# First adaLN modulation by blocks of 256 features on TensorE, first two in-projection tiles k-tile by k-tile, rotary sines moved into layer 0

## Chip, cores and metric

The kernel runs on one core of a Trainium2 chip. The metric is the device time of one execution, in microseconds (us). Before the change it is 2322.17 us, the median of three runs (2317.86 to 2325.34).

## What is computed

A decoder trunk of two layers over x (1024 tokens of 1024 features, f32). Cut to what the change touches, the reference is:

```
c_act = silu(c)                                    # 1024 values
for l in range(2):
    mod = c_act @ ada_w[l] + ada_b[l]              # 6 x 1024 values
    sh1, sc1, g1, sh2, sc2, g2 = split(mod, 6)
    h = rmsnorm(x, norm1_g[l]) * (1.0 + sc1) + sh1
    proj = h @ w_in[l]                             # in-projection, 20 tiles of 128 columns
    ...                                            # SSD, latent attention (rotary keys), window attention
    x = x + g1 * (y @ w_out[l])
    ...                                            # gated channel mixer
cos, sin = cos/sin(positions * inv_freq)           # for the rotary key and queries
```

Before the first in-projection tile can run, the kernel needs: x transposed, the inverse root mean square of each token, sh1 and sc1 of layer 0 (two column blocks of `ada_w[0]`, 8 MB), and the first tiles of `w_in`.

## The kernel before

The program is one block with five queues (SP issues the DMAs, TensorE, VectorE, ScalarE, GpSimd), each a hand-written order with semaphore waits. `first` fills the queues up to the first in-projection tile, `trunk_layer` follows once per layer; there is no barrier between them.

Every large matmul takes its operands as two fp32r parts, high and low (`wHi`, `wLo`, `hHi`, `hLo`), and makes three products (high by high, high by low, low by high). ScalarE writes the high part of a weight tile and GpSimd the low part (`split_ahead` for tiles 0 and 1, `split_pre` for the others). Tokens are the moving columns: two halves of 512.

`first` before the change:

- SP loads c, the rotary constants, eight x tiles (L539), then sixteen tiles of `ada_w[0]` (L536, 128 rows of 4 KB each: eight of sc1, then eight of sh1), then `w_in` tile 1. At its end it waits for the sines and stores cos and sin (L546).
- GpSimd fills constants, issues the loads of the positions, the parameters and `w_in` tile 0, and makes the low parts of tiles 0 and 1.
- TensorE transposes x (L595), the parameters (L434 to L439), takes four of the sixteen `ada_w` tiles as weights against one column of c_act (L603), and spreads the inverse norms into `bank[2]` (`spread_rms`, L480).
- ScalarE evacuates the x transposes (L623), squares x for the norms (L636), and makes the sines (L638, L644).
- VectorE works out the rotary angles (L662 to L673), multiplies and adds the other twelve `ada_w` tiles (L687, L690), folds them (L695, L696), and makes `mod` and `scl` (L680, L681, L703).

`trunk_layer` of layer 0 then makes h for the first 512 tokens, k-tile by k-tile: VectorE `nt = xT * scl * spread` (L2204, the spread read from PSUM), ScalarE `hHi` (L1807), VectorE `hLo` (L2213); then the same for the other 512 tokens. TensorE (L1184) runs in-projection tiles 0 and 1 on the first half, then on the second; tile 2 and the others follow by `dense_step` (L1124), over all 1024 tokens. Tile m uses `bank[m % 2]`, and TensorE waits on `pair_free0`/`pair_free1` until it is evacuated. For tiles 0 to 3 ScalarE alone evacuates. For tiles 4 to 11 ScalarE writes the convolution's base (L1874) and VectorE adds three taps from the bank (L2331), and only then the bank is free: so tile 6 waits for the taps of tile 4.

VectorE's own order in layer 0 after `hLo`: `early_products(0)` (the third modulation vector, eight tiles, L2265 and L2268), `step_sum`, `step_sizes` (which waits for a logarithm of ScalarE), `mod_fold(0)`, `early_products(1)`, `mod_fold(1)`, and then the taps of tile 4.

Of the kernel before, what the change touches and what calls it, by code (L numbers as in the profile page):

```python
# [129 lines left out]
ADA_BY_PE = (3, 7, 11, 15)  # L130
ADA_BY_DVE = (0, 1, 2, 4, 5, 6, 8, 9, 10, 12, 13, 14)
X_ACT = 8
# [46 lines left out]
def pv_end(u):  # L179
# [16 lines left out]
    "ada_prod": 14, "dve_step": 75, "n1_sq": 16, "n1_acc": 14, "n1_sum": 2, "n1_rstd": 4, "n1_spread": 2, "n1_scaled":  # L196
    24, "n1_hi": 24, "n1_lo": 24, "n2_sq": 16, "n2_acc": 14, "n2_sum": 2, "n2_rstd": 4, "n2_spread": 2, "n2_scaled": 16,
# [19 lines left out]
    "x_transposed": ("up_silu", NB), "x_copied_act": ("up_mul", X_ACT), "x_copied_dve": ("g_sums", NB - X_ACT),  # L217
    "c_transposed": ("dn_c", 1), "c_act": ("dn_copied", 1), "angle": ("dn_u", 1), "rope_sin": ("dn_pre", 2),
    "ada_done": ("dn_used", 14), "ada_sum": ("us_c", 6), "cs_stored": ("cum_loaded", 128)}
FIRST_ON.update({f"mod_loaded{i}": (name, 16) for i, name in enumerate(  # L220
    "dc_loaded0 dc_loaded1 dc_loaded2 g_stored0 g_stored1 g_stored2 x_back x_saved tail_loaded0 tail_loaded1 "
    "sd_row_stored sd_spread uproj_loaded cum_stored dt_stored dt_loaded".split())})
FIRST = {"dve_step": 16, "params_transposed": 1, "params_copied": 4, "mod_first": 2, "next_loaded1": 16, "next_hi": 2, "next_lo": 2, "next_swap": 2,
# [7 lines left out]
def build(nc, x, c, positions, ada_w, ada_b, norm1_g, norm2_g, w_in, ssd_conv_w, ssd_conv_b,  # L231
# [169 lines left out]
    def fview(t):  # L401
        return t.bitcast(F32)
# [87 lines left out]
    xin = [place(f"xin{i}", [P, D], F32, E[i]) for i in range(NB)]  # L490
    crow = place("crow", [8, P], F32, E[8])
    posi = place("posi", [P, T], I32, E[10])
    adaw = [place(f"adaw{i}", [P, D], F32, at["h"] + 4 * K * i) for i in range(2 * KT)]
    adas = [place(f"adas{g}", [P, D], F32, E[12 + g]) for g in range(2)]
    foldP = place("foldFirst", [P, 2, 32], F32, E[15])
# [27 lines left out]

    def first(block):

        def first_sums(a):

            return bank[3][:, 16:16 + 3 * KT] if a else bank[0][:, 0:3 * KT]

        @block.sync  # L530
        def _(sp):
            sp.dma_start(crow[:], c.rearrange("b (k p) -> (b k) p", p=P)).then_inc(s["small_loaded"], 16)
            sp.dma_start(ropec[:], rope_consts).then_inc(s["small_loaded"], 16)
            def load_adaw(i):
                g, k = 1 - i // KT, i % KT
                sp.dma_start(adaw[i][:], ada_w[0, k * P:(k + 1) * P, g * D:(g + 1) * D]).then_inc(s[f"mod_loaded{i}"], 16)  # L536
# [3 lines left out]
            for i in range(2 * KT):  # L540
                load_adaw(i)
# [2295 lines left out]
```

## Time and profile before

| | |
|---|---|
| Median of three runs | 2322.17 us |
| Span of the profiled execution | 2319.9 us |
| TensorE matmul busy | 2259.9 us (97%) |
| VectorE, ScalarE, GpSimd busy | 1633.3, 1102.8, 1021.4 us |
| First in-projection matmul | 47.85 us |
| Tile 2 begins | 72.40 us |

Times in the rows are microseconds from the start of the span. PE is TensorE's matmuls, PEld its weight loads, DVE VectorE, ACT ScalarE, POOL GpSimd, SPq the queue of SyncE. A row of a timeline gives start, duration, engine, line, operation and the tiles written and read; merged rows end with their count. The duration of an instruction that was held back while it ran includes that time. PEclk is the granted TensorE clock as a share of full speed (1.00 is 2.4 GHz, 0.50 is 1.2 GHz).

### The profile page before, as it was taken

The page shows a single profiled execution, that of the slowest core. Times are in us where ns is not written, and L with a number is a line of the kernel's source. Part 1 is how long each engine was busy: PE and PEld are TensorE (multiplying, and loading weights), DVE is VectorE, ACT ScalarE, POOL GpSimd, SP SyncE. Part 2 cuts the span into 40 slices and gives each one's busy share as a digit, 9 for nine tenths or more (in the row PEclk, how much of TensorE's full clock was granted, in tenths as well). Part 3 has the DMA queues.
Part 4 walks back from the last instruction along what each step waited for, and adds up shares of the span by engine and source line. Part 5 has one row for each costly group of instructions (what it writes and reads, how often), then busy time and mean ns, then how long its engine had stood idle before and what let it go on. Part 6 is the DMA issues. An engine that isn't in the chain of part 4 may idle for free.

```text
span 2319.9 us, 31032 instructions
## 1 busy us (share of the span) xinstructions
PE 2259.9 (97%) x11401; PEld 1853.4 (80%) x11401; DVE 1633.3 (70%) x2098; ACT 1102.8 (48%) x1817; POOL 1021.4 (44%) x660
## 2 busy tenths in 40 slices
PE   7999999999999999999999999999999999999998
PEld 6888867887788888888878787778878888888887
DVE  7985468449867666778888744772796767667886
ACT  5355557434444444444543464772454444444455
POOL 3222368445887777300012224053389777760000
PEclk7999999999999999999999999999999999999999
DMA  9742243242333333487466131114323333347763
GB/s 329 283 129 70 63 118 119 110 136 64 103 120 97 116 98 107 161 279 256 146 219 242 54 87 55 37 38 164 119 63 106 114 91 114 91 136 259 256 207 114
DMA packets 271301, 317.13 MB, mean 137 GB/s; under 512 B 33613, under 2 KB 188032, under 8 KB 270383
## 3 DMA queue, kind: packets, MB, share of 16 engines
q1 hardware_dynamic: 269359, 312.11, 41.7%
q10 hardware_dynamic: 1072, 2.23, 0.5%
q8 instruction: 91, 1.49, 0.3%
q0 software_dynamic: 720, 0.81, 0.1%
q14 instruction: 59, 0.48, 0.1%
HBM read 248.37 MB, written 62.54 MB: 134 GB/s over the span
## 4 chain that ended last, share of the span: by engine, by line
PE 84%; DVE 7%; issue 3%; ACT 2%; DMA 1%; SPq 1%; POOL 1%; DVEq 0%; ACTq 0%; POOLq 0%
PE bank L1561 31%; PE bank L1124 19%; PE bank L1576 17%; PE bank L1184 6%; PE bank L1343 1%; PE bank L1424 1%; DVE hLo L2227 1%; PE bank L1452 1%; ACT swaProb L1948 1%; SPq L536 1%; DVE xT L2221 1%; DMA adaw<-in_ada_w_dram 1%; PE bank L1274 1%; DVE xT L2562 1%; DVE tLo L2631 1%
## 5 line engine op out<-in xcount | busy, mean ns | idle before, releaser
L1044 POOL TENSOR_TENSOR wLo<-raw,wHi 128x1024 fp32r<-128x1024 f32 x66 | 161.2, 2443 | 408.6 <-ACT wHi L1046 408.6
L1754 POOL TENSOR_TENSOR prodLo<-comb,prodHi 128x512 fp32r<-128x512 f32 x160 | 233.9, 1468 | 122.4 <-ACT prodHi L1086 122.4
L1561 PE MATMUL bank<-tHi,prodHi 128*128 128x512 f32 x640 | 250.5, 391 | 4.8 <-DVE tLo L2631 4.1
L1561 PE MATMUL bank<-tLo,prodHi 128*128 128x512 f32 x640 | 250.0, 391 | 0.0
L1561 PE MATMUL bank<-tHi,prodLo 128*128 128x512 f32 x640 | 249.8, 390 | 0.0
L1576 PE MATMUL bank<-gateHi,downHi 128*128 128x512 f32 x616 | 240.6, 391 | 0.0
L1576 PE MATMUL bank<-gateHi,downLo 128*128 128x512 f32 x616 | 240.0, 390 | 0.0
L1576 PE MATMUL bank<-gateLo,downHi 128*128 128x512 f32 x616 | 239.9, 390 | 0.0
L1086 ACT ACTIVATE prodHi<-comb 128x512 fp32r<-128x512 f32 x160 | 100.5, 632 | 248.9 <-PE bank L1561 231.2
L2576 DVE SCALAR_TENSOR_TENSOR ub<-bank,ffp,ub 128x1023 f32<-128x1023 f32 x88 | 112.8, 1282 | 141.8 <-ACT ub L2034 140.2
L1561 PE MATMUL bank<-hHi,prodHi 128*128 128x512 f32 x480 | 187.3, 390 | 6.3 <-POOL prodLo L1754 3.7
L1561 PE MATMUL bank<-hHi,prodLo 128*128 128x512 f32 x480 | 187.0, 390 | 0.0
L1561 PE MATMUL bank<-hLo,prodHi 128*128 128x512 f32 x480 | 187.0, 390 | 0.0
L1124 PE MATMUL bank<-hHi,wHi 128*128 128x512 f32 x576 | 184.9, 402 | 0.0
L1124 PE MATMUL bank<-hLo,wHi 128*128 128x512 f32 x576 | 178.3, 391 | 0.0
L1124 PE MATMUL bank<-hHi,wLo 128*128 128x512 f32 x576 | 177.5, 390 | 0.0
L1046 ACT ACTIVATE wHi<-raw 128x1024 fp32r<-128x1024 f32 x66 | 69.6, 1057 | 219.9 <-PE bank L1124 144.9
L1754 POOL TENSOR_TENSOR prodLo<-raw,prodHi 128x512 fp32r<-128x512 f32 x120 | 164.7, 1398 | 0.0
L1561 PEld LDWEIGHTS bank<-tHi,prodHi 128*128 128x128 f32 x640 | 120.5, 188 | 31.5 <-DVE tLo L2631 5.0
L1561 PEld LDWEIGHTS bank<-tHi,prodLo 128*128 128x128 f32 x640 | 120.6, 188 | 25.2
L1561 PEld LDWEIGHTS bank<-tLo,prodHi 128*128 128x128 f32 x640 | 120.6, 188 | 24.7
L1576 PEld LDWEIGHTS bank<-gateHi,downHi 128*128 128x128 f32 x616 | 115.7, 188 | 24.7 <-issue 0.8
(424 smaller groups left out, 5434.9 us busy)
## 6 DMA issues: line engine op xcount, KB each, us to landing
raw<-in_ffn_w_up_dram SPq DMA_DIRECT2D x88, 512.0 KB, 4.7
gateRaw<-gateOut SPq DMA_DIRECT2D x154, 256.0 KB, 4.2
adaE<-in_ada_w_dram SPq DMA_DIRECT2D x64, 512.0 KB, 6.6
gateOut<-gateSums SPq DMA_DIRECT2D x22, 1024.0 KB, 5.5
raw<-in_w_in_dram SPq DMA_DIRECT2D x34, 512.0 KB, 4.1
downRaw<-in_ffn_w_down_dram SPq DMA_DIRECT2D x66, 256.0 KB, 3.6
raw<-in_w_out_dram SPq DMA_DIRECT2D x28, 512.0 KB, 3.8
downCols<-in_ffn_w_down_dram SPq DMA_DIRECT2D x24, 512.0 KB, 3.7
```

The costliest lines, as they stand in the source:

```text
L536: sp.dma_start(adaw[i][:], ada_w[0, k * P:(k + 1) * P, g * D:(g + 1) * D]).then_inc(s[f"mod_loaded{i}"], 16)
L1044: eng.tensor_tensor(lo[:], raw[slot][:], fview(hi[:]), ALU.subtract).then_inc(s["split_lo"], 1)
L1046: eng.activation((early_hi if n in (N_OUT0, N_PRE + 2) else third_hi if n == 2 else wHi[slot])[:], raw[slot][:], ACT.Copy).then_inc(s["spl ...
L1086: act.activation(sHiW[idx][:], product_source(js, idx), ACT.Copy).then_inc(s["us_hi"], 1)
L1124: last = mm(half(pair, hf), w(k), r(k)[:, HALF * hf:HALF * (hf + 1)], start=first and q == 0, stop=last_k and q == 2)
L1184: last = mm(o, w[n % 2][:, k * P:(k + 1) * P], r(k)[:, cols], start=first and q == 0, stop=last_k and q == 2)
L1274: last = mm(o, xd[:, h, :], Mt[g][:, q, :], start=True, stop=True)
L1343: last = mm(half(to, hf), wuq[:, k, t, :], cq[:, k, HALF * hf:HALF * (hf + 1)], start=k == 0, stop=k == 1)
L1561: last = mm(o, w[idx][:, c0], moving(idx, kp, hi), start=kp == 0 and q_ == 0, stop=kp == 3 and q_ == 2)
L1576: last = mm(down_bank(p, m), w[ring(n)][:, m * P:(m + 1) * P], g[ring(n)][:], start=i == 0 and q == 0, stop=i == NK - 1 and q == 2)
L1754: pool.tensor_tensor(sLoW[idx][:], product_source(js, idx), fview(sHiW[idx][:]), ALU.subtract).then_inc(s["us_lo"], 1)
L2576: dve.scalar_tensor_tensor(out=y[:, d:T], in0=bank[2 * q + b][:, 0:T - d], scalar=ffp[:, col:col + 1], in1=y[:, d:T], op0=ALU.mult, op1=AL ...
```

## The change

- **Loads.** The sc1 and sh1 parts of `ada_w[0]` come as eight transfers of 1 MB (all 1024 rows, 256 features, 1 KB pieces), sc1 block 0, sh1 block 0, then `w_in` tile 1, then blocks 1 to 3. The positions are loaded after `w_in` tile 0.
- **Modulation.** TensorE multiplies c_act, broadcast to 32 columns, by each block (`mod_products`: 16 plain f32 matmuls of 256 columns for a pair of blocks, each written to one of four groups of 32 partitions). ScalarE copies the sums out (`mod_rows`), TensorE transposes them (`mod_columns`), and VectorE reduces and adds the bias for two k-tiles of `mod` and `scl`. This goes four times; the first is in `first`, the other three stand inside the first two in-projection tiles.
- **h.** `xhat = x * spread` is made once for all 1024 tokens: k-tiles 0 to 3 by VectorE from PSUM, 4 to 7 by GpSimd from a copy in `nt[2]`. Then ScalarE makes `hHi` from it with scale and bias, and VectorE `nt = xhat * scl` and `hLo`.
- **Tiles 0 and 1** run over k-tiles, both tiles and both halves at each k, with the products of the next block after tile 0 of k = 0, 2, 3 and its transposes after tile 1.
- **Evacuation of the x transposes** goes from ScalarE to VectorE.
- **Sines.** The angles are worked out by VectorE after the last `hLo`, ahead of `early_products(0)`; the sines by ScalarE before its tile 2; the store of cos and sin stands before SP's `w_in` tile 5. `w_in` tiles 2 and 3 are issued before the wait for the modulation.

```diff
+    def mod_products(pe, b):
+        for n, g in enumerate(MOD_ORDER):
+            pe.wait_ge(s[f"mod_loaded{2 * b + n}"], 16)
+            if b:
+                pe.wait_ge(s["mod_row"], 2 * b)
+            for k in range(KT):
+                j = k % 4
+                last = pe.matmul(bank[3][32 * j:32 * j + 32, 256 * g:256 * g + 256], cact[:, k:k + 1].to_broadcast([P, 32]), adaw[g][b][:, k, :],
+                                 start=k < 4, stop=k >= 4)
+            last.then_inc(s["mod_made"], 1)
...
         @block.gpsimd
-            for n in range(AHEAD):
-                split_ahead(pool, n)
+            pool.dma_start(posi[64:128, :], positions.to_broadcast([64, T])).then_inc(s["pos_loaded"], 16)
+            split_ahead(pool, 0)
+            pool.wait_ge(s["spread_copied"], 1)
+            for k in range(X_BY_DVE, KT):
+                if k == X_BY_DVE + 1:
+                    split_ahead(pool, 1)
+                pool.tensor_tensor(xhat[k][:], xT[:, k, :], nt[2][:], ALU.mult).then_inc(s["xhat_pool"], 1)
...
         @block.scalar
+            act.wait_ge(s["n1_spread"], 1)
+            act.wait_ge(s["xhat_dve"], 2)
+            act.activation(nt[2][:], bank[2][:], ACT.Copy).then_inc(s["spread_copied"], 1)
             split_ahead(act, 0)
+            for b in range(MOD_BLOCKS):
+                mod_rows(b)
+                if b == 0:
+                    split_ahead(act, 1)
+                act.wait_ge(s["mod_first"], b + 1)
+                for k in range(2 * b, 2 * b + 2):
+                    act.wait_ge(s["xhat_dve" if k < X_BY_DVE else "xhat_pool"], k + 1 if k < X_BY_DVE else k + 1 - X_BY_DVE)
+                    act.activation(hHi[:, k, :], xhat[k][:], ACT.Identity, bias=mod[:, k:k + 1], scale=scl[:, 0, k:k + 1]).then_inc(s["n1_hi"], 1)
...
         @block.vector
+            for b in range(MOD_BLOCKS):
+                dve.wait_ge(s["mod_turned"], b + 1)
+                link(dve.tensor_reduce(both, bank[3][:, HALF:T].rearrange("p (g i j r) -> p g i j r", g=2, i=2, j=4)[:, :, :, :, 0], AX.X, ALU.add))
+                link(dve.tensor_tensor(both, both, prm[:, R_ADAB:R_ADAB + 2 * KT].rearrange("p (g k) -> p g k", g=2)[:, :, cols], ALU.add))
+                dve.scalar_tensor_tensor(out=scl[:, 0, cols], in0=mod[:, KT + 2 * b:KT + 2 * b + 2], scalar=1.0, in1=prm[:, R_N1 + 2 * b:R_N1 + 2 * b + 2],
+                                         op0=ALU.add, op1=ALU.mult).then_inc(s["mod_first"], 1)
+                for k in range(2 * b, 2 * b + 2):
+                    dve.tensor_scalar(nt[k % 2][:], xhat[k][:], scl[:, 0, k:k + 1], None, ALU.mult).then_inc(s["n1_scaled"], 1)
+                for k in range(2 * b, 2 * b + 2):
+                    dve.wait_ge(s["n1_hi"], k + 1)
+                    dve.scalar_tensor_tensor(out=hLo[:, k, :], in0=nt[k % 2][:], scalar=mod[:, k:k + 1], in1=fview(hHi[:, k, :]),
+                                             op0=ALU.add, op1=ALU.subtract).then_inc(s["n1_lo"], 1)
...
+            if not layer:
+                for k in range(KT):
+                    for t in range(2):
+                        pe.wait_ge(s["n1_lo"], nth("n1_lo", k + 1))
+                        last = dense_step(t, k, tile_of(t, wHi), tile_of(t, wLo), h_hi, h_lo, k == 0, k == KT - 1)
+                        if k in MOD_AT:
+                            (mod_columns if t else mod_products)(pe, MOD_AT.index(k) + 1)
...
-            for hf in range(1 if layer else 0, 2):
-                if layer:
-                    dve.wait_ge(s["n1_spread"], nth("n1_spread", 0))
-                norm1_apply(hf, n1_done(hf, -1), begun=not hf)
+            if layer:
+                dve.wait_ge(s["n1_spread"], nth("n1_spread", 0))
+                norm1_apply(1, n1_done(1, -1))
+            else:
+                rope_angles(dve, link)
```

## Rows read from the trace of the kernel before

**Rows 1.** The page, part 1: busy time, share of the span, instructions

```profile
PE 2259.9 (97%) x11401; PEld 1853.4 (80%) x11401; DVE 1633.3 (70%) x2098; ACT 1102.8 (48%) x1817; POOL 1021.4 (44%) x660
```

**Rows 2.** Chain of waits of the first 330 us: start, us, what

```profile
24.47 16.56 DMA adaw<-in_ada_w_dram
41.08 3.58 PE bank L603 x16
...
47.85 24.71 PE bank L1184 x96
72.56 62.56 PE bank L1124 x276
```

**Rows 3.** Stretches: length, busy of each engine, PEclk, DMA share, GB/s

```profile
24.00:26.00 2.00, 0.91 (x7) 0.71 (x9) 1.77 (x2) 2.00 (x5) 0.00 (x0) 0.72 1.02 406
...
52.00:54.00 2.00, 2.00 (x9) 1.60 (x9) 1.93 (x4) 0.86 (x2) 0.00 (x0) 0.95 1.02 395
```

**Rows 4.** DMA issues at 5.6 to 6 and 6 to 7 us: size, us to landing

```profile
xin<-in_x_dram SPq DMA_DIRECT2D x1, 512.0 KB, 12.6
...
adaw<-in_ada_w_dram SPq DMA_DIRECT2D x2, 512.0 KB, 15.3
```

**Rows 5.** Timeline of TensorE, first stage: start, us, engine, line, operation

```profile
21.29 1.06 PE L595 MATMUL bank<-ident,xin 128*128 128x128 f32 x8 [0.89 <-ACT xT L623]
...
34.32 1.97 PE L480 MATMUL bank<-ident,rst 128*128 128x128 f32 x8 [0.60 <-DVE rst L699]
```

**Rows 6.** Groups by line and shape: busy us, mean ns of one

```profile
L2460 DVE TENSOR_TENSOR swaProb<-bank,band 128x1024 f32<-128x1024 f32 x14 | 17.1, 1220 | 4.0 <-PE bank L1383 3.7
...
L687 DVE TENSOR_SCALAR adas<-adaw,cact 128x1024 f32<-128x1024 f32 x2 | 1.5, 748 | 0.0
...
L476 ACT ACTIVATE wHi<-raw 128x1024 fp32r<-128x1024 f32 x4 | 4.2, 1054 | 10.7 <-DMA raw<-in_w_in_dram 10.6
```

**Rows 7.** Timelines of VectorE and GpSimd at 69 to 79 us

```profile
68.94 0.75 DVE L2265 TENSOR_SCALAR nt<-adaE,cact 128x1024 f32<-128x1024 f32 x1
...
69.72 3.30 DVE L2268 SCALAR_TENSOR_TENSOR nt<-adaE,cact,nt 128x1024 f32<-128x1024 f32 x1
73.06 1.28 DVE L2268 SCALAR_TENSOR_TENSOR nt<-adaE,cact,nt 128x1024 f32<-128x1024 f32 x1
...
69.10 2.84 POOL L1044 TENSOR_TENSOR thirdLo<-raw,thirdHi 128x1024 fp32r<-128x1024 f32 x1 [23.12 <-DVE hLo L2213]
75.61 2.39 POOL L1044 TENSOR_TENSOR wLo<-raw,wHi 128x1024 fp32r<-128x1024 f32 x1 [3.66 <-ACT wHi L1046]
```

**Rows 8.** The same timelines at 562 to 569 us, both queues full

```profile
563.38 2.77 DVE L2569 SCALAR_TENSOR_TENSOR xT<-xT,mod 128x512 f32<-128x512 f32 x1
566.07 2.89 DVE L2562 TENSOR_TENSOR xT<-xT 128x512 f32<-128x512 f32 x1
...
562.76 8.46 POOL L1758 TENSOR_TENSOR tLo<-xT,tHi 128x1024 fp32r<-128x1024 f32 x3
```

**Rows 9.** Timeline of TensorE: plain f32 matmuls, output 128, 64, 32 wide

```profile
195.30 0.60 PE L1260 MATMUL bank<-xbc 128*128 128x128 f32 x4
...
197.95 1.09 PE L1274 MATMUL bank<-Mt,xdt 128*64 128x128 f32 x16 [0.67 <-DVE Mt L2377]
...
178.86 0.31 PE L1201 MATMUL bank<-foldMod,quadSum 128*32 128x32 f32 x8
```

**Rows 10.** Timeline of VectorE: first and last of 10 angle operations

```profile
12.59 0.69 DVE L663 CAST nt<-posi 64x1024 f32<-64x1024 int32 x1
...
22.52 0.69 DVE L673 TENSOR_SCALAR nt<-nt 64x1024 f32<-64x1024 f32 x1
```

**Rows 11.** Timeline of VectorE in layer 0, and tile 5's stretch

```profile
87.24 0.22 DVE L2244 TENSOR_SCALAR cs<-cs 64x128 f32<-64x128 f32 x1 [4.01 <-ACT cs L1902]
...
108.69 3.91 DVE L2331 SCALAR_TENSOR_TENSOR xbc<-bank,prm,xbc 128x1023 f32<-128x1023 f32 x3
...
105.04:115.92 10.88, 10.88 (x50) 9.02 (x48) 10.65 (x9) 2.16 (x2) 2.40 (x1) 1.00 0.72 255
```

## Prediction made before the change was run

> **What bounds the kernel now.** I read the page's busy shares first, then the chain of waits, then the timelines of the first 120 us. TensorE is busy for 97% of the span [rows 1], and from the first in-projection matmul on the chain stays on it: tiles 0 and 1 from 47.85 us, tile 2 from 72.40 us [rows 2] (the chain merges its first matmul, its piece begins at 72.56). So a microsecond won or lost before tile 2 is one of the whole, if nothing gives way later. Ahead of 47.85 us the chain is a DMA: the last `ada_w` tile lands at 41.08 us, and its matmuls, VectorE's fold and the first h follow [rows 2]. That is what the change attacks. The profiled span is 2319.9 us, the median of the runs 2322.17, so 2.3 us are added to a sum made on the span. About 7 us (0.3%) is what a measurement of this kernel can tell from no change.
>
> **Part 1: up to the first matmul.** The last x tile is issued at 5.4 us and lands 12.6 us later, at about 18.1 [rows 4]. Its pair is transposed in 2 x 1.06 us [rows 5], to 20.2; VectorE copies the last one out of PSUM (1.22, as for any 1024 columns read there [rows 6]), to 21.7. The parameter transposes take about 1.3 us (0.9 to 1.7 by the clock), to 23, and the eight spreads 1.0 to 2.0 [rows 5]: spread ready at 24.4 (23.6 to 25.4). The first two `ada_w` tiles land at 21.4 (6.1 + 15.3 [rows 4]) and the sixteenth at 41.08 [rows 2], that is 1.31 us for each 512 KB, so block 0 (2 MB) is there at about 25. Its products take 3.4 us at half clock (part 2), to 28.5; the clock is 0.72 at 24 to 26 us, already falling [rows 3].
>
> Meanwhile VectorE makes xhat 0 and 1 (2 x 1.25), to 26.9; ScalarE copies the spread (1.05 [rows 6]), to 28.1, and splits tile 0 (1.6 with its two small copies), to 29.7. Then come the rows (0.7) and TensorE's four transposes, to 31.9, and the reduce, to 32.1. GpSimd makes the low part of tile 0 (2.39 [rows 7]) until 32.2.
>
> **Now the new wait.** From 32.2 GpSimd has five operations in its queue: xhat 4, low part of tile 1, xhat 5, 6, 7, each two SBUF tensors of 1024 columns, so 2.39 us each [rows 7]. VectorE needs five before `hLo` 0 is done: bias add and scl (0.18 each), two `tensor_scalar` (0.78 with the gap, [rows 6]) and `hLo` (1.31 with the gap [rows 7]), all on SBUF alone. Such operations exclude each other here: a 1.28 us operation of VectorE lasted 3.30 while GpSimd's ran, and GpSimd's own, begun under a 0.75 us `tensor_scalar`, lasted 2.84 instead of 2.39 [rows 7]. With both queues full they take turns: 0.75 us operations of VectorE lasted 2.77 and 2.89, and three of GpSimd 8.46 [rows 8]. So four of GpSimd's five go between VectorE's: 32.2 + 4 x 2.39 + 2 x 0.18 + 2 x 0.78 + 1.31 = 45.0 us for the first matmul. Without turns it would be 35.6. Before it was 47.85. The gain here is 2.9 us (by the spread's bounds 1.9 to 3.7; by another phase of the turns down to -1), not 12.
>
> The Trainium skill ("SBUF — State Buffer", section "SBUF: two separate sides") says the same from the other side: one port pair of VectorE and GpSimd is an exclusive lock, held for the whole instruction, asked for by a VectorE operation with two SBUF inputs or in its 2-port mode. It speaks against this change, which puts five GpSimd operations where VectorE's chain stands. Were the two `tensor_scalar` free of it, contrary to the page, the first matmul would come at 38.7.
>
> **Part 2: tiles 0 and 1.** Before, they took 24.55 us (47.85 to 72.40), 96 matmuls with the first 4 us at half clock [rows 2, 3]. The same matmuls and the same ramp remain, now with these in the queue:
> - Three times 16 plain f32 matmuls of 256 columns with 32 output partitions. A plain f32 matmul is two instructions. With 128 output partitions, those of 128 columns come every (0.60 - 0.27) / 3 = 0.11 us; with 64, in alternate halves, 16 take 1.09, one per 0.055; with 32, in four groups, eight of 32 columns begin within 0.08 us, which is one per 0.012 [rows 9] (0.27 and 0.23 are the lengths of one). So groups run beside each other. At 256 columns one alone is 0.213. Four at once: 32 / 4 x 0.213 = 1.7 us a block. Two at once 3.4, one after another 6.8. I take 1.7, since the row with four groups is of this form; 3.4 is the upper end. Cost 3 x 1.7 = 5.1 us (up to 10.2).
> - Three times four transposes, 0.5 each: 1.5 us.
> - After the first block's transposes VectorE needs about 3.6 us (0.6, two 0.78, 1.31) before k-tile 2, and TensorE has 2.7 us of k-tile 1: 0.9 us idle. Later blocks are ahead.
>
> Sum 32.05, so tile 2 begins at 77.05, not 72.40: +4.65 us. ScalarE and GpSimd split tile 2 after `hLo` 7 (about 71), within 3.5 us: in time.
>
> The Trainium skill ("TensorE: Matmul & The Clock Gate", section "Part 3: Packing small matmuls — row/col tiling") measured 2.38 times for three column tiles, not 3. By an estimate from that page a block would be 2.1 us and tile 2 would begin 1.2 us later still.
>
> **Part 3: the sines in layer 0.** The angle operations take 10.6 us on VectorE (12.59 to 23.21 [rows 10]). They ran while the loads were awaited, but VectorE's chain after them was as long as the loads. Now they stand between `hLo` 7 and `early_products(0)`. Queued behind them: both early products, `step_sum` (for which ScalarE then waits at tile 2, about one us past its next split), the step sizes, and the taps of tile 4, for which TensorE waits at tile 6. Before, the taps ended at 112.6 and tile 6 began at 115.92 [rows 11]: 3.3 us of slack. The balance, relative to the start of tile 2: +10.6 angles; -2.7, as `hLo` 7 ends 6.1 us ahead of tile 2 and not 3.4; -2.4, as VectorE no longer idles 4.01 us for the logarithm [rows 11] but about 1.6; +4.2 for two more splits of GpSimd (tiles 4 and 5 or 6) which now meet VectorE busy with two SBUF inputs, 2.1 each (3.30 - 1.28 [rows 7]); -3.3 slack. Stall at tile 6: 6.4 us (2 without the meetings, 8.5 if the idle time stays). Once tile 6 is delayed, each later tile gives VectorE 10.88 us [rows 11] for about 9 of work, so I expect it once only. ScalarE's two sine operations and a table load (about 3.5 us) stand before its split of tile 4, where it waited for TensorE: 0 us, up to 1 if the angles come late. SP: the store of cos and sin waits for the sines and `w_in` tile 5 stands behind it, needed some 20 us later: 0. The earlier issue of tiles 2 and 3: 0, neither was waited for; it puts `ada` loads of layer 0 behind the modulation, 20 us later than before, still ahead of VectorE.
>
> **Sum.** 2319.9 - 2.85 + 7.5 + 6.4 = 2331.0 on the span; with 2.3 around it 2333 us, that is +11.
>
> **Rivals.**
> 1. *Not slower: the turns don't happen at the start and the lag is absorbed.* GpSimd's operations would have to fall between VectorE's instead of ahead of each. First matmul at 35.6, tile 2 at 67.6, no stall: -4.8 us, 2317.4. It decides from a first matmul earlier than 40.4 us with no idle at tile 6. If besides the clock stayed full (the ramp costs some 2 us), 2315. For it: [rows 3] shows the clock lost only where TensorE was sparse. Against it: [rows 7, 8].
> 2. *No turns at the start, but the lag.* 2317.4 + 6.4 = 2323.8. For it: the operations at the start have small ones among them, which may slip through.
> 3. *Turns at the start, lag absorbed.* 2322.17 + 4.65 = 2326.8. For it: 2.4 us of VectorE's slack at the logarithm and 3.3 at tile 6; it needs GpSimd's splits to miss VectorE.
> 4. *Column groups run two at a time.* Block 0 at half clock takes 6.8, the first matmul comes at 47.4, and three blocks cost 5.1 us more: 2333.2 + 7.5 = 2340.7. For it: the pair row; against it: the row with four groups [rows 9].
>
> **How the numbers follow.** Forecast 50%, own range 2329 to 2337; rival 1: 7%; rival 2: 13%; rival 3: 15%; rival 4: 13%; 2% for what I have not seen. The range of 8 in 10 leaves out most of rival 1 and the top of rival 4: 2319 to 2341. Faster by over 0.3% (below 2315.2): the best tail of rival 1 and something unseen, 6%. Slower by over 0.3% (above 2329.1): 47 of the forecast's 50, rival 4, and 2 of the others: 62%. Within: 32%.
>
> **What would show it.** Right: GpSimd's xhat operations back to back from about 32 us with VectorE's 0.18 and 0.75 us operations lasting 2.4 to 3.2 between them; first matmul at 45; tile 2 at 77; products of a block in 1.7 us; an idle of some 6 us of TensorE before tile 6, ended by VectorE's third tap of tile 4. Wrong: a first matmul before 41 (part 1), products of 3.4 us (part 2), no idle before tile 6 (part 3). A spread later than 26 us would move everything with it.

## The result, and the profile after

The changed kernel takes 2341.03 us (median of four runs, 2338.88 to 2342.15) against 2322.18 us before: a ratio of 1.0082, 95% interval 1.0068 to 1.0096, or +19 us. The prediction was 2333 (+11) with a range of 2319 to 2341, so the sign was right and the size was 8 us short. The profiled execution has a span of 2337.1 us, 17.2 more than the one before.

TensorE's busy time hardly moved. This is the page, part 1 (it answers to [rows 1]):

```profile
PE 2251.4 (96%) x11465; PEld 1839.2 (79%) x11465; DVE 1630.6 (70%) x2085; ACT 1099.1 (47%) x1811; POOL 1032.4 (44%) x664
```

So the 17 us are idle time and slow clock, and it is enough to look for TensorE's waits. The chain of waits of the changed kernel answers to [rows 2] (start, us, what):

```profile
64.64 9.59 PE bank L1138 x42
74.25 1.04 ACT misc L1917
75.31 13.79 DMA dtOut<-misc
89.11 2.48 DMA cs<-dtOut
...
106.08 11.42 DMA adaE<-in_ada_w_dram
...
136.05 9.02 PE bank L1138 x30
```

Before, one piece of TensorE ran from 72.56 us on. Now the chain leaves TensorE at 74 us and comes back at 136. Two kinds of DMA stand in it that the chain before did not have: a 32 KB store of dt that took 13.8 us, with its reload, and a late load of the fourth modulation vector. The timeline of TensorE shows the three places where it stood (first matmul of tiles 0, 3 and 6), and the first matmul of tile 2:

```profile
42.23 1.19 PE L1138 MATMUL bank<-hHi,wHi 128*128 128x512 f32 x2 [12.73 <-DVE hLo L717]
...
75.42 0.70 PE L1138 MATMUL bank<-hHi,thirdHi 128*128 128x512 f32 x2
...
94.00 1.22 PE L1138 MATMUL bank<-hHi,wHi 128*128 128x512 f32 x2 [7.41 <-POOL wLo L1058]
...
136.05 1.19 PE L1138 MATMUL bank<-hHi,wHi 128*128 128x512 f32 x2 [6.68 <-DVE xbc L2364]
```

Each stall also costs clock. By stretches (length, busy of TensorE, PEclk, DMA share, GB/s):

```profile
94.00:98.00 4.00, 4.00 (x10) 0.50 0.00 0
98.00:100.00 2.00, 2.00 (x8) 0.70 0.90 203
...
136.00:140.00 4.00, 3.95 (x9) 0.50 1.05 315
```

After these waits of 7.4 and 6.7 us, TensorE runs at half clock (1.2 GHz) for 4 to 5 us. From tile 3's first matmul (94.00) to tile 6's turn (136.05 - 6.68 = 129.37) three tiles took 35.4 us; at 10.88 each [rows 11] they need 32.6: 2.7 us for the clock. After tile 6 it is 2.1: a fixed set of products later (`foldMod`, 178.86 us before) starts 65.0 us after tile 6's first matmul, before the change 62.9.

| | before | after | difference |
|---|---|---|---|
| First in-projection matmul | 47.85 | 42.23 | -5.6 |
| Tile 2 begins | 72.40 | 75.42 | +3.0 |
| Stall at tile 3, and its clock | 0 | 7.4 + 2.7 | +10.1 |
| Stall at tile 6, and its clock | 0 | 6.7 + 2.1 | +8.8 |
| `foldMod` products begin | 178.86 | 201.05 | +22.2 |
| Layer 1, `swaV` transposes | 1436.93 | 1457.17 | +20.2 |
| Span | 2319.9 | 2337.1 | +17.2 |

The terms give 3.0 + 10.1 + 8.8 = 21.9 of the 22.2. The last two rows of the table say that 2 us come back between 201 and 1457 us and 3 after that. The 3 are the clock of these two executions: over the 63 us from the `swaV` transposes of layer 1 the granted clock was 0.92 before (1437 to 1500 us) and 1.00 after (1457 to 1520 us), which is 5 us. Where the 2 are I have not found; both are of the size by which runs differ.

### The profile page after: what moved, and what is told of

Read it like the earlier page. It is cut to its first block, busy times and chain, and to the rows that moved or that the text cites. A ratio compares the mean times of both kernels' runs of the same rounds, so it can differ in the third digit from the quotient of the medians.

```text
span 2337.1 us, 31167 instructions
## 1 busy us (share of the span) xinstructions
PE 2251.4 (96%) x11465; PEld 1839.2 (79%) x11465; DVE 1630.6 (70%) x2085; ACT 1099.1 (47%) x1811; POOL 1032.4 (44%) x664
## 4 chain that ended last, share of the span: by engine, by line
PE 81%; DVE 8%; issue 3%; ACT 3%; DMA 2%; POOL 1%; SPq 1%; DVEq 0%; ACTq 0%; POOLq 0%
PE bank L1588 30%; PE bank L1138 17%; PE bank L1603 17%; PE bank L1198 5%; PE bank L1370 1%; PE bank L1451 1%; DVE hLo L2257 1%; ACT swaProb L1979 1%; PE bank L1479 1%; DVE xT L2251 1%; DMA raw<-in_ffn_w_up_dram 1%; PE bank L1288 1%; DVE xT L2595 1%; DMA dtOut<-misc 1%; DVE tLo L2664 1%
## 5 line engine op out<-in xcount | busy, mean ns | idle before, releaser
L1058 POOL TENSOR_TENSOR wLo<-raw,wHi 128x1024 fp32r<-128x1024 f32 x66 | 161.8, 2452 | 431.4 <-ACT wHi L1060 431.4
L1138 PE MATMUL bank<-hHi,wHi 128*128 128x512 f32 x608 | 198.1, 407 | 27.4 <-DVE hLo L717 13.3
L1138 PE MATMUL bank<-hLo,wHi 128*128 128x512 f32 x608 | 190.3, 394 | 0.0
L1138 PE MATMUL bank<-hHi,wLo 128*128 128x512 f32 x608 | 189.0, 392 | 0.0
L1138 PEld LDWEIGHTS bank<-hHi,wHi 128*128 128x128 f32 x608 | 111.4, 191 | 50.4 <-issue 21.7
L1588 PEld LDWEIGHTS bank<-tLo,prodHi 128*128 128x128 f32 x640 | 120.2, 188 | 24.6
```

The costliest lines, as they stand in the source:

```text
L1058: eng.tensor_tensor(lo[:], raw[slot][:], fview(hi[:]), ALU.subtract).then_inc(s["split_lo"], 1)
L1138: last = mm(half(pair, hf), w(k), r(k)[:, HALF * hf:HALF * (hf + 1)], start=first and q == 0, stop=last_k and q == 2)
L1588: last = mm(o, w[idx][:, c0], moving(idx, kp, hi), start=kp == 0 and q_ == 0, stop=kp == 3 and q_ == 2)
```

## Where the waits come from: reading the trace

The row `[7.41 <-POOL wLo L1058]` says that GpSimd's low part of tile 3 ended the wait. GpSimd had itself waited for ScalarE's high part, and ScalarE for a DMA of its own. ScalarE's timeline after the change:

```profile
75.31 0.57 ACTq L1921 DMA_DIRECT2D dtOut<-misc  x1
...
89.11 0.53 ACTq L1924 DMA_DIRECT2D cs<-dtOut  x1
89.75 1.06 ACT L1060 ACTIVATE wHi<-raw 128x1024 fp32r<-128x1024 f32 x1 [12.79 <-DMA dtOut<-misc]
```

and before:

```profile
71.62 0.55 ACTq L1890 DMA_DIRECT2D dtOut<-misc  x1
...
73.51 0.52 ACTq L1893 DMA_DIRECT2D cs<-dtOut  x1
74.47 1.06 ACT L1046 ACTIVATE wHi<-raw 128x1024 fp32r<-128x1024 f32 x1 [0.84 <-issue]
```

The same store took 1.9 us before and 13.8 now. What had changed around it is in the timeline of SP's queue. After:

```profile
65.27 3.96 SPq L845 DMA_DIRECT2D adaE<-in_ada_w_dram  x8
69.28 0.44 SPq L888 DMA_DIRECT2D xtail<-xT  x1
...
97.30 3.90 SPq L576 DMA_DIRECT2D csOut<-cs  x8
...
101.95 4.61 SPq L845 DMA_DIRECT2D adaE<-in_ada_w_dram  x8
```

and before:

```profile
46.03 3.90 SPq L835 DMA_DIRECT2D adaE<-in_ada_w_dram  x8
...
55.86 3.28 SPq L876 DMA_DIRECT2D xtail<-xT  x1
...
78.53 3.88 SPq L835 DMA_DIRECT2D adaE<-in_ada_w_dram  x8
```

SP waits for `mod_first`, the signal that the modulation of layer 0 is made, ahead of eight loads (`adaE`, the third modulation vector, 4 MB). Before, that wait ended at 46 us; now the last block of the modulation is made at 65, so these loads and the 4 MB save of x behind them (`xtail`) start 5 to 10 us before ScalarE's 32 KB store. The second group of `adaE` loads, for the fourth vector, stands behind the store of cos and sin, that behind the sines, those on ScalarE behind the dt round trip: 101.95 us instead of 78.53.

My theory after reading this: (1) the stall at tile 3 is the dt store behind the 8 MB; (2) the stall at tile 6 is the late loads of the fourth vector. The rival for (2) was the prediction's own: VectorE's lag from the angle operations.

## The experiments

Stalls are read from TensorE's timeline or waits of each profile; "at 2322" is the ratio's excess times 2322 us. All compare with the kernel before.

| | change made to | ratio (95%) | at 2322 | tile 2 begins | stall tile 3 | stall tile 6 |
|---|---|---|---|---|---|---|
| the change | | 1.0082 (1.0068-1.0096) | +19 | 75.42 | 7.4 | 6.7 |
| e1 | change: saves early | 1.0046 (1.0032-1.0061) | +10.7 | 76.12 | 0 | 6.0 |
| e2 | change: split first | 1.0106 (1.0093-1.0119) | +24.6 | 73.90 | 0 (4.3 at tile 4) | 13.7 |
| e3 | change: no angles | 1.0096 (1.0083-1.0110) | +22.3 | 75.37 | 6.5 | 7.5 |
| e4 | change: xhat on VectorE | 1.0080 (1.0068-1.0092) | +18.6 | 66.75 | 7.9 | 11.2 |
| e5 | before: saves late | 1.0030 (1.0015-1.0046) | +7.0 | 71.69 | 0 (0.8 at tile 4) | 5.0 |
| e6 | e1, no angles | 1.0034 (1.0023-1.0045) | +7.9 | 75.12 | 0 | 3.8 |
| e7 | e6, cos/sin store last | 1.0014 (1.0004-1.0024) | +3.3 | 76.44 | 0 | 0 |
| e8 | change: all mended | 0.9993 (0.9982-1.0004) | -1.6 | 67.11 | 0 | 0.3 |
| e9 | change: dt on GpSimd | 1.0103 (1.0088-1.0118) | +23.9 | 75.03 | 0.8 (0.9 at tile 4) | 15.4 |
| e10 | change: save of x early | 1.0056 (1.0044-1.0069) | +13.0 | 74.52 | 0 | 8.6 |

**e1: SP's save and early loads ahead of its wait.**

```diff
                         load_pack(3, kind, 3)
-                        sp.wait_ge(s["mod_first"], nth("mod_first", 0))
-                    load_early(0, range(KT), 0)
+                        sp.wait_ge(s["x_copied"], NB)
+                        sp.dma_start(xtail, xT[:]).then_inc(s["tail_saved"], 16)
+                        load_early(0, (0, 1, 2, 3, 5, 6, 7), 0)
+                        sp.wait_ge(s["mod_turned"], MOD_BLOCKS)
+                        load_early(0, (4,), 0)
...
```

> The changed kernel, with SP's 4 MB save of x and its eight loads of the third modulation vector issued before its wait for the whole first modulation (some 45 us) instead of after it (65.3 to 69.7 us). Theory: TensorE's 7.4 us at tile 3 are ScalarE's wait for its own 32 KB store of dt, which took 13.8 us because 8 MB were queued ahead of it; the store should land in about 2 us, the split of tile 3 come at about 77 instead of 89.8, and the 7.4 us go. The 6.7 us at tile 6 should go too, since the early loads of the fourth vector, which they wait for, are issued some 12 us sooner (at most 1 us left by VectorE's own queue): 2341.0 - 7.4 - 6.7 = 2327, bounds 2326 to 2329. Rival A, the sum of the prediction, in which VectorE's lag behind the angle operations makes the stall at tile 6 by itself: 7.4 go, 6.4 stay, 2334. Rival B, the store of dt is slow for another reason: no change, 2341.

Measured: 1.0046. Tile 3 no longer waits; from ScalarE's, VectorE's and TensorE's timelines of e1:

```profile
76.01 0.56 ACTq L1926 DMA_DIRECT2D dtOut<-misc  x1
...
77.86 0.52 ACTq L1929 DMA_DIRECT2D cs<-dtOut  x1
78.49 1.06 ACT L1065 ACTIVATE wHi<-raw 128x1024 fp32r<-128x1024 f32 x1 [0.84 <-DMA dtOut<-misc]
...
107.44 0.75 DVE L2301 TENSOR_SCALAR nt<-adaE,cact 128x1024 f32<-128x1024 f32 x1 [1.04 <-DMA adaE<-in_ada_w_dram]
...
125.96 0.77 PE L1143 MATMUL bank<-hHi,wHi 128*128 128x512 f32 x1 [6.04 <-DVE xbc L2369]
```

The store is back at 1.9 us and the first part of the theory holds. The second does not: the loads of the fourth vector were issued 10 us sooner (91.57) and tile 6 still waited 6.0 us. Rival A, the prediction's sum, came out in size: +10.7 for +11, and 6.0 us of stall for 6.4. But the loads are not out of the way in e1. VectorE was free for the fourth vector's products at 106.4 us and waited 1.04 us more for their loads, so the loads set the 6.0, and VectorE's own lag stands just behind them, at about 5.0. That the two are so close is a coincidence. What I had missed is the difference between e1 and the change.

**e3: without nine of the angle operations** (cos and sin are not the reference's).

```diff
-        link(dve.tensor_scalar(ang[lo, :], ang[lo, :], ropec[lo, 0:1], None, ALU.mult))
-        ...
-        link(dve.tensor_scalar(ang[lo, :], ang[lo, :], ropec[lo, 2:3], None, ALU.add))
```

> The changed kernel without nine of the eleven angle operations on VectorE (the conversion and the last clamp stay; 8.3 us less work; the angles, and so cos and sin, are not the reference's). Theory: in the changed kernel VectorE waits 9.5 us for the loads of the fourth vector after this work, so taking it away moves nothing: tile 3 waits 7.4, tile 6 waits 6.7, 2341 within 1 us. Rival, the step of the prediction (VectorE's lag behind the angles makes the stall at tile 6): the stall at tile 6 goes, 2334.5.

Measured: 1.0096, no gain; 6.5 and 7.5 us of stall, as the theory said. VectorE, 9 us earlier at the products of the third vector, waited 5.95 us for those loads (to 78.8 us) and then 10.0 us for the fourth's. So neither e1, which makes the loads 10 us sooner, nor e3, which takes the angles out, changes the stall at tile 6 by as much as 1 us. Two causes side by side would do that: whichever is reduced, the other is as late.

**e6 and e7: both causes removed.** e6 is e1 with e3's edit; e7 also moves the store of cos and sin behind the fourth vector's loads:

```diff
-                if kind == "win" and m == 5 and not layer:
+                if kind == "win" and m == 6 and not layer:
                     store_rope(sp)
```

> e1_saves_early, also without nine of the eleven angle operations (so cos and sin are not the reference's). In e1 TensorE still waited 6.0 us at tile 6; VectorE began the products of the fourth vector at 107.4, 1.0 us after it was free and when its loads had landed. Theory (two causes of about the same size stand behind the wait at tile 6, VectorE's lag and the loads of the fourth vector, issued behind the store of cos and sin): with the lag gone the loads alone remain, which move up by the 3 us that the sines waited for the angles: 2 to 4 us of wait at tile 6, 2329 to 2331. Rival (the lag alone): no wait, 2327.

> e6, with SP's store of cos and sin moved behind the loads of the fourth vector. Theory of two causes: both are gone, no wait at tile 6 and none at tile 3: e1 minus 6.0, that is 2327. Rival (the tile waits for something else, for instance ScalarE or the weight loads): a wait of 2 us or more stays.

Measured: 3.8 us of stall in e6, none in e7; 1.0034 and 1.0014. VectorE's timelines show the step from one to the other: in e6 it still stood 7 us for the loads, in e7 not at all.

```profile
104.22 0.75 DVE L2292 TENSOR_SCALAR nt<-adaE,cact 128x1024 f32<-128x1024 f32 x1 [7.05 <-DMA adaE<-in_ada_w_dram]
```

```profile
98.41 0.75 DVE L2292 TENSOR_SCALAR nt<-adaE,cact 128x1024 f32<-128x1024 f32 x1
```

What remains of the change in e7, +3.3 us, is of the size of tile 2's later start (76.44 - 72.40 = 4.0). The run that has the lag alone, e1 with the store of cos and sin last and the angles kept, was not made; the 5.0 us above are read from e1's trace.

**e2: ScalarE splits tile 3 before it waits for the dt store.**

```diff
                     if m == 1:
+                        if not layer:
+                            split_pre(act, 3)
                         act.wait_ge(s["dt_stored"], nth("dt_stored", 16))
...
-                        split_pre(act, 3)
+                        if layer:
+                            split_pre(act, 3)
```

> The changed kernel, with ScalarE's split of tile 3 ahead of its wait for the store of dt in layer 0. Both theories: the 7.4 us of TensorE at tile 3 go, the store of dt still takes about 13.8 us. Theory: what follows on ScalarE (sines, store of cos and sin by SP, then the loads of the fourth vector) stays where it is in time, so tile 6 waits for what it waited for, now 7.4 us longer: a stall of 13 to 14 us at tile 6, the time within 1.5 us of 2341. Rival: the two stalls are independent, the one at tile 6 stays 6.7, 2333.6.

Measured: 1.0106. Tile 3 is in time and nothing is won: tile 6 waits 13.7 us, twice as long, as expected, and 4.3 us more stand at tile 4, whose split is behind ScalarE's wait for the reload and its sines. A stall that is removed where it shows, while its cause stays, moves to the next user.

**e5: the converse, on the kernel before.** SP's early loads and save start at about 65 us there too.

```diff
+                        load_pack(2, kind, 2)
+                        load_pack(3, kind, 3)
                         sp.wait_ge(s["mod_first"], nth("mod_first", 0))
+                        sp.wait_ge(s["n1_lo"], nth("n1_lo", n1_done(1, 4)))
                     load_early(0, range(KT), 0)
...
-                if n >= AHEAD:
+                if n >= (AHEAD if layer else 4):
```

> The kernel before, with one thing of the change: SP waits for the thirteenth low part of h (about 65 us) before it issues the eight loads of the third modulation vector and the save of x (before: 46.0 and 55.9 us); w_in tiles 2 and 3 go ahead of them. Theory (the store of dt waits for the 8 MB queued ahead of it): the store, issued at 71.6, takes some 14 us instead of 1.9, the split of tile 3 comes at about 86 and its low part at 89.4, against tile 3's turn at 83.3: TensorE waits about 6 us for it, 2328, bounds 2326 to 2334 (VectorE's 3.3 us of slack at tile 6 could be used up too). Rival (the delay at tile 3 needs something else of the change, the angles or GpSimd): no wait at tile 3, 2322.

Measured: 1.0030, +7 us, the size expected but not the place. From ScalarE's and VectorE's timelines of e5:

```profile
70.91 0.56 ACTq L1893 DMA_DIRECT2D dtOut<-misc  x1
...
77.58 0.52 ACTq L1896 DMA_DIRECT2D cs<-dtOut  x1
...
87.93 0.40 ACT L1899 ACTIVATE cs<-cs,prm 64x128 f32<-64x128 f32 x1 [8.34 <-DMA cs<-dtOut]
...
78.38 0.75 DVE L2268 TENSOR_SCALAR nt<-adaE,cact 128x1024 f32<-128x1024 f32 x1 [10.08 <-DMA adaE<-in_ada_w_dram]
```

Here the store took 6.7 us and the reload 10.4; in the changed kernel 13.8 and 2.5. The sum, 16 to 17 us, is about the same, so the longer round trip needs nothing else of the change. The split of tile 3 stands between the two, and it was in time. The 5.0 us at tile 6 are not the round trip's: VectorE waited 10.1 us for the loads of the third vector and was through with their products 7.3 us later than before (90.3 for 83.0), when the reload had already landed, and the load of `w_in` tile 4, issued behind the save of x, took 20.4 us instead of 3.8 and held ScalarE's next split until 91.25. So e5 got the expected size by another way. It shows that moved loads can be late for their own user too; in the changed kernel the angle operations, which VectorE does first, hid that.

**e10 and e9: how much is ahead, and which queue.** e10 moves only the save of x (e1's first two lines). e9 has GpSimd issue the store and the reload:

```diff
+                if n == 2 and not layer:
...
+                    pool.wait_ge(s["pair_free0"], nth("pair_free0", 1))
+                    pool.dma_start(dt_out[0]...).then_inc(own["first_pos"], 16)
+                    pool.wait_ge(own["first_pos"], 32)
+                    pool.dma_start(draw_dt, ...).then_inc(own["first_pos"], 16)
...
+                            act.wait_ge(own["first_pos"], 32)
+                            split_pre(act, 3)
+                            act.wait_ge(own["first_pos"], 48)
```

> The changed kernel, with only the 4 MB save of x moved ahead of SP's wait for the modulation; the eight loads of the third vector (4 MB) are still issued at 65.3 to 69.2. If the store of dt waits for what is queued ahead of it, it waits for 4 MB instead of 8: about 10 us from 65.3 for them by 400 GB/s, so it lands at 77 to 79, 2 to 4 us after its issue, in time for tile 3 (turn at 86.3). TensorE's wait at tile 3 goes, that at tile 6 stays at 6 to 7: 2333 to 2334, as e1. Rival (a delay that any load before it brings, whatever its size): some 13 us of wait, 2341.

> The changed kernel, with the store and the reload of dt in layer 0 issued by GpSimd, whose DMAs have a queue of their own (q0 in the table of queues; those of SP and ScalarE are both in q1). The 8 MB of SP stay where they are, and ScalarE still waits for the store before it splits tile 3. Theory A (the small store waits its turn behind the 8 MB in the same queue): it lands some 5 us after its issue, as GpSimd's small loads do at the start of the kernel while SP's 4 MB are under way, that is at about 81; the split of tile 3 is in time (its low part at 85, tile 3's turn is 86.3), the 7.4 us at tile 3 go and a wait of 6 to 8 us at tile 6 stays: 2333 to 2335. Theory B (the transfer itself is slow because the 16 DMA engines are full): it lands at 88 as before, 2341.

Measured: e10 1.0056, the stall at tile 3 gone, 8.6 us at tile 6 (6 to 7 expected). Two of GpSimd's splits, 3.24 and 3.45 us, fell among VectorE's products of the third vector (13.24 us for seven, 9.21 in the change), but VectorE then still waited 3.7 us for the loads of the fourth, so those set the 8.6. e9 1.0103, slower than the 2333 to 2335 of theory A and the 2341 of theory B: the stall at tile 3 is down to 0.8 us, but 15.4 us stand at tile 6, where VectorE waited 9.8 us for the loads of the fourth vector, as in e2. One premise of e9 was false. The table of queues shows SP's DMAs in q1 and ScalarE's in a queue of their own already (queue, kind: packets, MB, share of the 16 engines; changed kernel, 60 to 95 us):

```profile
q1 hardware_dynamic: 2336, 8.91, 66.5%
q10 hardware_dynamic: 152, 0.07, 0.7%
```

So the store was never behind the 8 MB in one queue, and a third queue helps little: 7.9 us for the store and 6.4 for the reload, 14.3 together instead of 16.3. What goes with the round trip in all the kernels is how long SP's bulk transfers (the loads of the third vector and the save of x) are under way. By stretches (length, busy of TensorE, PEclk, DMA share, GB/s), the changed kernel and then e10:

```profile
80.00:85.00 5.00, 5.00 (x24) 1.00 0.99 423
85.00:90.00 5.00, 1.58 (x7) 0.90 0.85 320
```

```profile
75.00:80.00 5.00, 5.00 (x23) 1.00 0.73 247
80.00:85.00 5.00, 5.00 (x24) 1.00 0.02 7
```

The store's time is from its issue to the issue of the reload:

| | store issued | store, us | reload, us | reload landed |
|---|---|---|---|---|
| before | 71.6 | 1.9 | 2.6 | 76.1 |
| e1 | 76.0 | 1.9 | 2.1 | 80.0 |
| e10 (4 MB ahead) | 74.4 | 5.8 | 2.0 | 82.2 |
| the change (8 MB) | 75.3 | 13.8 | 2.5 | 91.6 |
| e5 (8 MB) | 70.9 | 6.7 | 10.4 | 87.9 |
| e9 (8 MB, GpSimd's queue) | 75.6 | 7.9 | 6.4 | 89.9 |

e2, e3 and e4, with the 8 MB in the same place as the change, have 15.1 + 2.1, 13.7 + 2.2 and 14.9 + 2.8 us. The save of x landed 20.7 to 21.0 us after its issue in the last three of the table, at about 90. So theory A of e9 falls: it is not the order within one queue. Theory B's cause, DMA engines that are full, fits the table, though its number was off (the store landed at about 83, not 88). e10 and the change differ in the save alone: without it the store is back at 80.2, with it at 89.1. Both kinds of bulk are not told apart by a run: the save writes to DRAM as the store does, the loads read from it, and no run has the save late and the loads early, so whether the amount counts or the kind is open. How an engine picks between the queues is open too, and so is why the slow half is now the store and now the reload. The Trainium skill ("DMA: Bandwidth & Descriptors", section "Queues, rings and completion order") says that each engine takes turns between the queues packet by packet. From that I would estimate that the store's 76 small packets (half of q10's 152) slip through in a few us; 6.7 to 15.1 us were measured on ScalarE's queue beside the 8 MB, so here the rule alone is too hopeful. In "Rules for kernel authors" the same page of the Trainium skill says that spreading DMAs over issuing engines doesn't help bandwidth, since all run on the same 16 DMA engines. It speaks of bandwidth and not of one small transfer; e9, where another issuing engine made the round trip only 2 us shorter, is in line with it.

**e4: the turns at the start.** VectorE makes all of xhat, two ahead of each block; GpSimd keeps only its two splits.

```diff
-X_BY_DVE = 4
+X_BY_DVE = KT
...
-            for k in range(X_BY_DVE, KT):
-                ...
-                pool.tensor_tensor(xhat[k][:], xT[:, k, :], nt[2][:], ALU.mult)
+                for k in range(2 * b + 2, min(2 * b + 4, KT)):
+                    make_xhat(k)
```

> The changed kernel with all eight normalised k-tiles made by VectorE, two ahead of each block (1.25 us each), and none by GpSimd, which keeps only the low parts of tiles 0 and 1. Theory of the turns: of the four GpSimd operations (2.39 each) that stand between VectorE's add and the first low part of h only one is left (low part of tile 1), so the first matmul comes at about 36.2 instead of 42.2 us; VectorE's chain of a block (2.5 + 0.6 + 1.6 + 2.6 = 7.3 us) fits into TensorE's 8 us, so tile 2 begins 5 to 6 us earlier, at 69.5 to 70.5, and all later things of SP and ScalarE move with it: 2335 to 2336. Rival: the wait before the first matmul isn't made by turns but by the modulation's own chain; then the first matmul stays at 41 to 43 and the time at 2341 or above, as VectorE has 5 us more work.

VectorE's timeline of the changed kernel, and GpSimd's beside it:

```profile
29.82 1.10 DVE L705 TENSOR_TENSOR mod<-mod,prm 128x4 f32<-128x4 f32 x1
30.96 2.26 DVE L706 SCALAR_TENSOR_TENSOR scl<-mod,prm 128x2 f32<-128x2 f32 x1
33.26 5.55 DVE L713 TENSOR_SCALAR nt<-xhat,scl 128x1024 f32<-128x1024 f32 x2
38.73 6.66 DVE L717 SCALAR_TENSOR_TENSOR hLo<-nt,mod,hHi 128x1024 fp32r<-128x1024 f32 x2
...
30.86 2.34 POOL L620 TENSOR_TENSOR xhat<-xT,nt 128x1024 f32<-128x1024 f32 x1
33.16 2.35 POOL L468 TENSOR_TENSOR wLo<-raw,wHi 128x1024 fp32r<-128x1024 f32 x1
```

The same in e4:

```profile
29.52 2.17 DVE L706 TENSOR_TENSOR mod<-mod,prm 128x4 f32<-128x4 f32 x1
31.72 0.16 DVE L707 SCALAR_TENSOR_TENSOR scl<-mod,prm 128x2 f32<-128x2 f32 x1
31.91 1.42 DVE L714 TENSOR_SCALAR nt<-xhat,scl 128x1024 f32<-128x1024 f32 x2
33.27 2.48 DVE L718 SCALAR_TENSOR_TENSOR hLo<-nt,mod,hHi 128x1024 fp32r<-128x1024 f32 x2
...
34.71 1.19 PE L1141 MATMUL bank<-hHi,wHi 128*128 128x512 f32 x2 [5.50 <-DVE hLo L718]
```

With GpSimd's queue full each of VectorE's operations waits for one of GpSimd's; the two that take 0.16 to 0.17 us alone take 1.10 and 2.26, and the four large ones 5.55 and 6.66 where e4 has 1.42 and 2.48. Without them the first matmul comes at 34.7 instead of 42.2. Tile 2 begins 8.7 us sooner than in the change, and yet the time is the same (1.0080). The expectation, that later things move along, was wrong: tile 3 waits 7.9 us, and tile 6 11.2, since the loads of the fourth vector landed only 6.6 us sooner (110.9 for 117.5) and two low parts of GpSimd fell among its products (13.35 us for seven of them, 11.22 before). Tile 6 begins at 131.6, 4.5 us sooner than in the change, and these 4.5 don't show in the time. The traces tell where they went: the `swaV` transposes of layer 0 still begin 3.8 us sooner (323.09 for 326.87), those of layer 1 no longer (1457.43 for 1457.17). In between, by slices of 10 us, the granted clock of e4 fell to 0.94, 0.72, 0.97 and 0.86 from 340 to 380 us and to 0.87 and 0.79 from 420 to 440, that of the change only once, to 0.83 (350 to 360), which is 6.8 us more lost in e4, enough for them. Why it fell there in one execution and not in the other is open.

**e8: all three mended, kernel complete.** e1 + e4 + e7's order of SP, with the angle operations spread over VectorE's gaps between blocks (four ahead of the first, then three, one, none and three) in scratch of their own; `next(angles)` runs the next group.

```diff
+            angles = rope_angles(dve, link)
+            next(angles)
...
+                next(angles)
```

> The changed kernel, complete, with the three causes taken away: saves early (e1), normalised k-tiles on VectorE (e4), the store of cos and sin behind the loads of the fourth vector, and the angle operations in the gaps of VectorE between the blocks (four before the first block's columns arrive, three after it, one after the second, three after the last). Theory: first matmul at 34.7 as in e4, tile 2 at 67.5 to 68, no wait at tiles 3 and 6: e1 (2333) minus 9.0 (43.7 to 34.7) minus 6.0 is 2318, bounds 2316 to 2322, which is rival 1 of the prediction. Rival: the operations in the gaps delay the blocks (1.3 us each for up to two) and a wait of 2 us or more at tile 6 stays: 2322 to 2325.

Measured: 0.9993 (0.9982 to 1.0004), at 2322 us 2320.5. First matmul 35.09, tile 2 at 67.11, and the only stall left is 0.3 us at tile 6. That is about 20 us better than the change, and no different from the kernel before by this measurement. The profiled execution was a quick one (span 2313.7). The prediction's rival 1 gave 2317.4, just below the interval (2318.0 to 2323.1): about what the change would give if nothing behind it were late.

## Why the prediction was right, and where it was wrong

**Part 1, first matmul: right in mechanism, 2.8 us too late** (45.0; 42.2 measured, 40.9 to 44.1 in the profiles of e1 to e3, e6, e7, e9 and e10, which have the same code there). The turns are there: four of GpSimd's operations stand between its low part of tile 0 and `hLo` 0, as predicted, and the two `tensor_scalar` are held too (2.8 us each for 0.75). Taking GpSimd's xhat operations away (e4) moved the first matmul by 7.5 us. The trace agrees with the Trainium skill's rule ("SBUF — State Buffer", "SBUF: two separate sides") in that the two engines exclude each other for whole instructions. The sum was too high in its beginning: the products of block 0 took 1.07 us for each half at full clock, not 3.4 for both at half clock, GpSimd was through with the low part of tile 0 at 30.9, not 32.2, and VectorE's add started at 29.8, not 32.2. That the clock was full there is particular to this execution: e1 to e4 and e7 to e10 have about 1.94 for each half, and their first matmul is within the same 40.9 to 44.1 where GpSimd makes xhat. One side number does not follow from the prediction's own rule: with the two `tensor_scalar` free, `hLo` 0 would still wait for a third operation of GpSimd, and the first matmul would come at 32.2 + 3 x 2.39 + 0.36 + 1.31 = 41.0, not 38.7.

```profile
23.76 1.07 PE L532 MATMUL bank<-adaw,cact 128*32 128x256 f32 x16 [0.35 <-DMA adaw<-in_ada_w_dram]
26.61 1.07 PE L532 MATMUL bank<-adaw,cact 128*32 128x256 f32 x16 [1.78 <-DMA adaw<-in_ada_w_dram]
```

**Part 2, tiles 0 and 1: 32.05 predicted, 33.2 measured.** A block of products at full clock took

```profile
55.40 1.93 PE L532 MATMUL bank<-adaw,cact 128*32 128x256 f32 x32
```

against 1.7; the estimate from the Trainium skill ("TensorE: Matmul & The Clock Gate", "Part 3: Packing small matmuls — row/col tiling") was 2.1, and the measurement lies between. The first block after the wait for h ran mostly at half clock (3.36), which the sum had at full clock. Four column groups do run side by side, so rival 4 is out. Tile 2's start at +3.0 instead of +4.65 is the sum of both parts.

**Part 3, VectorE's lag: there, but behind another cause.** The prediction gave it 6.4 us at tile 6. By e1's trace it is about 5.0 by itself, with 1.0 more from the loads; in the changed kernel the late loads stand in front of it altogether (VectorE waited 9.5 us for them, after the lag). That the stall in the changed kernel is 6.7, near the 6.4, is luck: the sum was right for a wait that another cause ended. e6 and e7 show that the loads make 3.8 us without the angles, and that the stall is gone with both. "Once only" held. Missing in the sum is the clock after a stall, put at nothing and measured as 2.1 and 2.7 us. (The upper value of 8.5 is 6.4 + 2.4 = 8.8 by the prediction's terms.)

**The step that failed** is one sentence: the early issue of tiles 2 and 3 "puts `ada` loads of layer 0 behind the modulation, 20 us later than before, still ahead of VectorE", with the price 0. The sentence is true in the changed kernel: VectorE found them in time (81.75 us, no wait), though by 3 us only, going by e3, where they ended its wait at 78.8. It asks only who uses the moved data, not what else is under way in the new place. There, 8 MB keep the DMA engines busy from 65 to 90 us, and ScalarE's two 32 KB transfers, with a split behind each, stand in that stretch. That is 7.4 + 2.7 us in the changed kernel; e1 prices the whole of it at 8.4 us (1.0082 - 1.0046) of 2322, give or take 5 by the two intervals. The error of the forecast adds up so: -1.65 from parts 1 and 2, +10.1 at tile 3, +2.4 at tile 6 (8.8 for 6.4), together +10.9, of which 8 are left in the measured time. The second sentence of this kind was "`w_in` tile 5 stands behind it, needed some 20 us later: 0": it was SP's next item behind that, the fourth vector's loads, that came 23 us late and held tile 6: the chain goes from the dt round trip over the sines, their store and these loads to VectorE's products and the taps. They would have held it without VectorE's lag too (e3).

**The rivals.** Rivals 2 and 3 left out one of two costs that both came. Rival 1's time was reached only by the edits of e8; in the change itself neither of its conditions held. None of the rivals had a transfer as its mechanism. That the range ends close to the result is rival 4's doing, which did not happen.

## What to carry to other kernels

When a wait on the DMA-issuing queue moves, list every transfer behind it, and for each new place ask what small transfers with a waiting engine share the DMA engines there, not only whether the moved data are in time. Two causes that end at the same tile hide each other: remove them singly and together before either is called harmless, and look at what ends the wait even where the size comes out as expected (e1 and e5 here). And a stall of TensorE cost more than its idle time here: 2.1 and 2.7 us of half clock behind stalls of 6.7 and 7.4.

## What the runs showed of the hardware that I had not expected

- A round trip of 32 KB (store and reload) of 3.9 to 4.5 us took 15.9 to 17.7 us on ScalarE's queue while 8 MB of SP's queue were under way at some 400 GB/s, 14.3 us on GpSimd's queue, and 7.8 us on ScalarE's with 4 MB of loads. Which half of it is slow varies (13.8 + 2.5, 6.7 + 10.4, 7.9 + 6.4).
- VectorE's operations of 0.16 us on a few columns last up to 2.26 us beside GpSimd's large ones (2.35 us), as its large operations are held too. In the dependent chain ahead of the first `hLo` each operation of VectorE, small or large, cost about one of GpSimd's.
- Sixteen plain f32 matmuls of 256 columns (32 instructions in the trace) in four column groups take 1.93 us at full clock: 0.24 us for four instructions, against the prediction's estimate of 0.213 if they overlapped wholly.
